# Conditioning slabs dealt over the first layer's value projection: six, then twelve late and close together, in place of eight and ten

## The reference

```python
cs = jax.nn.silu(c)
mod = (cs @ ada_w[l] + ada_b[l])[:, None, :]
sh_a, sc_a, g_a, sh_m, sc_m, g_m = jnp.split(mod, N_MOD, axis=-1)
h = x * (1.0 + sc_a) + sh_a
y = gla_mixer(h, ...)            # projections q, k, v, r, gate; chunks of 64; out projection
x = layer_norm(DEEPNORM_ALPHA * x + (1.0 + g_a) * y, ln_g[l, 0], ln_b[l, 0])
h = x * (1.0 + sc_m) + sh_m
y = sq_relu_mlp(h, mlp_w1[l], mlp_b1[l], mlp_w2[l], mlp_b2[l])
x = layer_norm(DEEPNORM_ALPHA * x + (1.0 + g_m) * y, ln_g[l, 1], ln_b[l, 1])
```

## Time and profile before

| | us |
|---|---|
| median of 3 executions | 2267.72 (2265.85 to 2270.01) |
| the profiled execution, its device time | 2266.52 |
| the same, its span in the trace | 2264.8 |
| PE busy in it | 2231.1 |
| DVE busy | 1724.1 |
| ACT busy | 1136.3 |

### The profile page before, as it was taken

How to read it: one execution, slowest core, us unless ns; L and a number is a source line. 1 busy time by engine, 2 the same in 40 slices (tenths; PEclk the granted TensorE clock), 3 DMA queues, 4 the chain that set the end, 5 groups by cost and what they waited for, 6 DMA issues and landing times.

```text
span 2264.8 us, 32117 instructions
## 1 busy us (share of the span) xinstructions
PE 2231.1 (99%) x10956; PEld 1876.0 (83%) x10956; DVE 1724.1 (76%) x1703; ACT 1136.3 (50%) x1408; POOL 19.0 (1%) x41
## 2 busy tenths in 40 slices
PE   7999999999999999999999999999999999999998
PEld 6786878888888888888888888888888888888886
DVE  6679789988888888898777867888766455556656
ACT  2144365565555554444555555545555555444443
POOL 1000000000000000000000000000000000000000
PEclk9999999999999999999999999999999999999999
DMA  9998999679999999979768766884877556766563
GB/s 393 418 374 313 348 392 392 227 282 378 376 380 375 379 372 346 339 246 353 283 222 324 271 240 232 314 316 143 306 287 267 186 191 203 254 194 190 194 208 125
DMA packets 146475, 658.61 MB, mean 291 GB/s; under 512 B 16496, under 2 KB 16816, under 8 KB 115792
## 3 DMA queue, kind: packets, MB, share of 16 engines
q1 hardware_dynamic: 144000, 642.05, 76.9%
q0 software_dynamic: 2384, 15.37, 1.7%
HBM read 655.22 MB, written 2.13 MB: 290 GB/s over the span
## 4 chain that ended last, share of the span: by engine, by line
PE 88%; DMA 6%; DVE 4%; issue 1%; SPq 1%; ACT 0%; DVEq 0%; ACTq 0%
PE ps L1427 19%; PE ps L1325 18%; PE ps L1326 17%; PE ps L1329 17%; PE ps L1429 10%; DMA R<-in_mods 3%; DMA mod_w<-in_mods 2%; DVE mod_w L874 1%; DMA raw<-in_tiles 1%; PE ps L1459 1%; PE ps L1583 0%; DVE stats L954 0%; PE ps L1528 0%; PE ps L1527 0%; PE ps L1529 0%
## 5 line engine op out<-in xcount | busy, mean ns | idle before, releaser
L869 DVE TENSOR_TENSOR w_lo<-raw,w_hi 128x1024 fp32r<-128x1024 f32 x720 | 877.0, 1223 | 448.1 <-ACT w_hi L435 444.7
L435 ACT ACTIVATE w_hi<-raw 128x1024 fp32r<-128x1024 f32 x720 | 760.1, 1059 | 831.7 <-PE ps L1329 375.5
L1325 PE MATMUL ps<-w_hi,h_both 128*128 128x512 f32 x1872 | 735.8, 393 | 3.3 <-ACT w_hi L435 3.3
L1326 PE MATMUL ps<-w_hi,h_both 128*128 128x512 f32 x1872 | 729.0, 389 | 0.0
L1427 PE MATMUL ps<-h_both,w_hi 128*128 128x512 f32 x1920 | 666.3, 391 | 0.0
L1429 PE MATMUL ps<-h_both,w_lo 128*128 128x256 f32 x1920 | 537.6, 280 | 0.0
L1329 PE MATMUL ps<-w_lo,h_both 128*128 128x512 f32 x1872 | 506.5, 390 | 2.4 <-DVE w_lo L869 2.4
L874 DVE SCALAR_TENSOR_TENSOR mod_w<-mod_w,cs 128x2048 f32<-128x2048 f32 x200 | 457.0, 2285 | 30.3 <-DMA mod_w<-in_mods 21.6
L1427 PEld LDWEIGHTS ps<-h_both,w_hi 128*128 128x128 f32 x1920 | 359.1, 187 | 79.0
L1325 PEld LDWEIGHTS ps<-w_hi,h_both 128*128 128x128 f32 x1872 | 351.5, 188 | 79.1 <-ACT w_hi L435 3.6
L1329 PEld LDWEIGHTS ps<-w_lo,h_both 128*128 128x128 f32 x1872 | 350.8, 188 | 78.1 <-DVE w_lo L869 5.1
(11 more groups left out here) (192 smaller groups left out, 1038.3 us busy)
## 6 DMA issues: line engine op xcount, KB each, us to landing
raw<-in_tiles SPq DMA_DIRECT2D x736, 512.0 KB, 4.7
mod_w<-in_mods SPq DMA_DIRECT2D x200, 1024.0 KB, 7.0
R<-in_mods SPq DMA_DIRECT2D x16, 1024.0 KB, 21.9
odd_raw<-in_tiles SPq DMA_DIRECT2D x16, 512.0 KB, 20.5
R<-in_tiles SPq DMA_DIRECT2D x16, 512.0 KB, 6.5
R<-in_ln_rows POOLq DMA_DIRECT2D x6, 1024.0 KB, 8.4
G<-in_mods SPq DMA_DIRECT2D x4, 1024.0 KB, 21.9
S<-in_mods SPq DMA_DIRECT2D x4, 1024.0 KB, 23.9
```

Of the source, the lines that this page charges most:

```text
L435: nc.scalar.activation(w_hi[:, slot, :], raw[:, slot, :], ACT.Copy).then_inc(hi_ready, 1)
L869: nc.vector.tensor_tensor(w_lo[:, slot, :], raw[:, slot, :], w_hi[:, slot, :].bitcast(F32), ALU.subtract)\
L1325: mm(dst, h_hi[:, kt, toks], w_hi[:, slot, c], start=start, stop=False, skip_group_check=more)
L1326: return mm(dst, h_lo[:, kt, toks], w_hi[:, slot, c], start=False, stop=False, skip_group_check=more)
```

## The change

The first body of V does 6 slabs in place of 8, the second 12 in place of 10; the sum of both is the same, and from V+32 on every list is as before. The first two slabs of V are multiplied ahead of V+0, before as now. The first body keeps its slabs at tiles 1, 3 and 4, and its fourth moves from tile 5 to tile 10; those that stood at 10 and 15 are dealt with the second body's. There the twelve stand by a list of their own: V+18, 20, 23, 24, 25, two at V+26, and one at each of V+27 to V+31. Before, the second body had them at V+17, 18, 20, 21, 23, 24, 26, 28, 29 and 31.

```diff
-SCHEDULE = [("gv", 0, 1, 8), ("gv", 16, 1, 10), ("gr", 0, 1, 12), ("gr", 16, 1, 8), ("go", 0, 1, 8), ("go", 16, 1, 2), ("u0", 0, 1, 0), ("u0", 16, 7, 8),
+SCHEDULE = [("gv", 0, 1, 6), ("gv", 16, 1, 12), ("gr", 0, 1, 12), ("gr", 16, 1, 8), ("go", 0, 1, 8), ("go", 16, 1, 2), ("u0", 0, 1, 0), ("u0", 16, 7, 8),
...
-        MODS_DONE = {T0["gv"]: {1: (2,), 3: (3,), 4: (4,), 5: (5,), 10: (6,), 15: (7,)}, T0["go"] + 16: GO_MODS}
-        MODS_LOADED = {T0["gv"]: {3: (2, 3), 4: (4,), 5: (5,), 10: (6,), 15: (7,)}, T0["go"] + 16: GO_MODS}
+        GV_MODS = {2: (0,), 4: (1,), 7: (2,), 8: (3,), 9: (4,), 10: (5, 6), 11: (7,), 12: (8,), 13: (9,), 14: (10,), 15: (11,)}
+        MODS_DONE = {T0["gv"]: {1: (2,), 3: (3,), 4: (4,), 10: (5,)}, T0["gv"] + 16: GV_MODS, T0["go"] + 16: GO_MODS}
+        MODS_LOADED = {T0["gv"]: {3: (2, 3), 4: (4,), 10: (5,)}, T0["gv"] + 16: GV_MODS, T0["go"] + 16: GO_MODS}
```

## The result

The change takes 2270.9 us (median of 14 executions, 2267.8 to 2273.43); the kernel before, run 14 times beside it, 2266.28 (2265.54 to 2270.01). The ratio is 1.0017 with a 95% interval of 1.001 to 1.0024: 4 to 5 us slower, where 3.2 us faster were forecast. The profiled execution took 2272.56, span 2270.8 against 2264.8, so what follows accounts for 6.0 us, of which the median shows 4.6.

What follows compares the result with a forecast made beforehand. PE was taken to bound the kernel, busy 2231.1 of 2264.8 us. An early gain of 8.8 us, less 5.6 given back, left 3.2 us off the median of 2267.72: 2264.5 us, range 2259.0 to 2270.5.

Steps and rivals of the forecast that it cites:

- 8.8 us are lost there: V+2 to V+26: PE has 76.5 us of work in 85.25; the change was to recover all 8.8 us.
- The thin places V+10, V+11 and V+14: Early tiles whose `w_hi` or `w_lo` was estimated ready only 0.3 to 0.5 us ahead of PE.
- the rival of the early waits: Early waits stay, PE reaches V+26 only some 2 us early; 2265.7 or up to 2268 us, chance 0.18.
- no sooner than 3.45 us behind the landing of its tile: At V+48, ACT's `w_hi`, table load and r columns hold PE's start 3.45 us behind the tile's landing.
- The 33.0 MB from 209.7 us: Queue's load from V+25's slab to V+48's tile, 23 tiles and 20 slabs, forecast to take 89.4 to 91.7 us.
- in the new order the queue is kept fed like this or slightly worse: Assumption for the queue up to V+48: old rates of 369 or 360 GB/s carry over to the new list.
- The 369: Queue rate in GB/s from 216.11 to 302.57 us without two short stretches; put V+48 4.3 us ahead.
- 5.6 of the 8.8 us are given back: Between V+31 and V+48, PE waits were to return 5.6 us of the early gain, leaving 3.2 us.
- Behind V+48 the gain holds: After V+48 nothing more is lost: V+56 has 0.9 us to spare, and beyond it every list is old.
- Full recovery: Rival: queue holds 390 GB/s or more from 209.7 us, nothing given back; gain 8.8 us, 2258.9 us, chance 0.13.
- Starved weights: Rival: slab waits leave the queue short from V+26; at 330 GB/s V+48 is 6.4 us late, 2274.1 us, chance 0.11.
- The limit from the Trainium skill: About 358 GB/s of HBM traffic per core; by it the queue's stretch takes 92.2 us and the gain is 1.5 us.

Runs made afterwards that it cites:

- e9: The change with four slab buffers in place of two from V+25 to V+41; 2258.3 us, 0.9962 of the kernel before.
- e4: The change, but DVE multiplies only half the columns of the slabs at V+18 to V+47, all bytes still loaded; 2261.64 us.
- e6: The change with four slab buffers in place of two from V+25 to V+31 only; 2263.43 us, 0.9981 of the kernel before.
- e5: The change with ten slabs, by the old list, in V's second body and two moved to the output projection's first body; 2268.17 us.
- e3: The change with the slab loads from V+23 to V+47 issued two tile loads later, products unmoved; 2275.45 us.
- e7: The change with ten slabs, by the old list, in V's second body and two moved to the r projection's second body; 2268.83 us.

## Why the prediction was wrong

- **"8.8 us are lost there"**, and the early gain of 8.8: right. V+26 was forecast at 227.5 and started at 227.78. The log-sigmoid was to start near 160.1; DVE's timeline has it at 160.15. The thin places V+10, V+11 and V+14 held, so the rival of the early waits fell.

```profile
160.15 2.29 DVE L1096 SCALAR_TENSOR_TENSOR R<-ps,R 128x2048 f32<-128x2048 f32 x1 [0.58 <-ACT R L646]
```

- **V+48 "no sooner than 3.45 us behind the landing of its tile"**: right. ACT's timeline has the `w_hi` at 307.46, straight behind the landing at 307.38, and the r columns from 309.83; PE starts at 310.91, 3.5 us behind the landing. ACT had been busy without a pause since 302.40, though, and came free just as the tile landed, so this trace does not tell which of the two was the last to hold V+48.

```profile
307.46 1.06 ACT L436 ACTIVATE w_hi<-raw 128x1024 fp32r<-128x1024 f32 x1
308.53 1.28 ACT L723 ACT_TABLE_LOAD   x1
309.83 1.03 ACT L723 ACTIVATE S<-ps 128x1024 f32<-128x1024 f32 x1
```

- **The 33.0 MB from 209.7 us**: the stretch and its start (the slab of V+25 issued at 207.82 in place of 207.4) were right, the rate was not. This is the step that failed: "in the new order the queue is kept fed like this or slightly worse". It took 97.7 us, 338 GB/s, against 360 to 369 assumed and 352 where it breaks even. V+48's tile landed at 307.38 in place of 299.1 to 301.4. The 369 had been cleaned of two short stretches in which SP was held by PE, but SP was held by slabs for 71.8 us of the same time, as shown above, and the list of the change only asks for more of them. What was missing is the loop. Its parts stood in the trace: a landing of at least 4.8 us, a product of 2.3. At their smallest they give (4.8 + 2.3) / 2 = 3.55 us per tile, 0.83 above PE's 2.72; over the seven tiles V+25 to V+31 that is 5.8 us, which the 11.2 us of the scores cover. At the measured 4.75 it is 14.2 us, which they don't: V+31 starts 4.3 us behind e9's, V+34 10.4. The longer landing could have been read beforehand too. The page of the kernel before has it as the median of 200 slabs, and (7.0 + 2.3) / 2 is 4.65:

```profile
mod_w<-in_mods SPq DMA_DIRECT2D x200, 1024.0 KB, 7.0
```

  A mean rate taken from a list in which slabs stand apart can't be carried to one in which they stand close. e4, e6 and e9 show this cause: the same list, with the loop loosened, gives 383, 387 and 408 GB/s.
- **"5.6 of the 8.8 us are given back"**: 12.6 were. In the trace 8.4 us of them are pauses of PE (83.13 us from V+26 to V+48, 74.73 busy in them); the rest is the low clock of V+30, 1.6 us, and late starts behind eight or so pauses, about 0.3 us each.
- **"Behind V+48 the gain holds"**: nearly. There was no gain to hold, but V+48 to V+56 took 22.4 us against 21.8, and V+72 to V+95 59.3 against 58.4, in lists that are unchanged. Why these two stretches lost 1.5 us was not tried.
- **Full recovery** is what the change makes of the early part if the queue is fed. That rival asked for 390 GB/s or more and gave 2258.9; e9 has 408 and 2258.3. **Starved weights** was the case that came true, for the reason that it names, at 338 GB/s in place of 330. Its chance of 0.11 was too small. The evidence against it (SP held by PE, not by a slab) was true of two short stretches, not of the whole of the past list.
- **The limit from the Trainium skill.** In the prediction, 358 GB/s stood as a possible ceiling, from the Trainium skill, "DMA: Bandwidth & Descriptors", section Specifications. e9 moved 408 GB/s over 90.3 us, so the trace disagrees: there was no such ceiling for this core. The same page of the Trainium skill, section Bandwidth, gives 425 GB/s for a load of 16 MB by one core alone, and keeps some 358 for the case that both cores of the pair stream. With this the trace's 408 agrees.

## What to carry to other kernels

When loads with few buffers are moved close together, work out the time of their loop (landing in a shared queue, plus the consumer, over the number of buffers) and set it against the pace of the engine that must be fed, before any mean rate is used. A mean rate holds only for the order in which it was measured. And work moved out of a full stretch needs a place where the queue has room: read the DMA share there first.

## What the runs showed of the hardware

- A 1 MB load landed in 4.8 us alone, 7.2 us (median of ten) in the change with one slab and some tiles beside it, and some 12 us in e9's full queue. The 7.2 was not expected of a queue that runs dry in between: a slab and a tile take 3.75 us at e9's rate. In the dip of the saw at 217.5 to 219 us the DMA share was 0.21 to 0.30, so most of the 16 DMA engines stood idle, while the slab issued at 211.73 was still under way (its product starts at 218.96). Why its last part comes so slowly stays open.
- TensorE's granted clock fell to 1.2 GHz in places, in the profiled execution of the change at V+30: eight matmuls took 3.49 us at a mean granted clock of 0.52, in place of 1.93 (227.78 to 229.71 in the timeline), behind a pause of 2.31 us. It did so behind 2.66 us in e5 (1.6 us lost) and behind 4.08 us in e3, but not behind 3.05 us at V+34 of the change or 2.23 us in e7. In the change this cost little, I think, since V+32 had to wait for its tile even so; it was not tried apart.
- The spread between executions differs from kernel to kernel: the change's 14 lie 5.6 us apart, e9's five 0.6. It does not simply follow PE's waits, since e6, with 0.6 us of them in its profile, has 6.5 us between its ten. What makes it stays open.
